# Block 1's last convolution taps beside its attentions; block 2's keys and values projected once, with the compression in the same stage

## The reference, cut to what matters

```python
def conv_branch(u_glu, u_gate, conv_w, conv_b, ln_g, ln_b, w_proj):   # block 1, beside two attentions
    a = u_glu[..., :D_CONV] * jax.nn.sigmoid(u_glu[..., D_CONV:])
    a = depthwise_conv(a, conv_w, conv_b)                             # 31 taps on 512 channels
    a = jax.nn.silu(layer_norm(a, ln_g, ln_b))
    return (a * jax.nn.silu(u_gate)) @ w_proj
...
def _compress(z, pe, w1, w2):                                         # block 2, on k_cmp and v_cmp
    zr = z.reshape(B, n_chunk, CMP_STRIDE, G, dh)
    blocks = jnp.concatenate([zr[:, j:j + nc] for j in range(r)], axis=2)
    blocks = blocks + pe[:, None, :]
    flat = blocks.transpose(0, 3, 1, 2, 4).reshape(B, G, nc, CMP_BLOCK * dh)
    return jax.nn.gelu(flat @ w1) @ w2
...
    k_cmp, v_cmp, k_slc, v_slc, k_win, v_win = [z.reshape(B, S, G, dh) for z in jnp.split(kv_a, 6, axis=-1)]
    kc = _compress(k_cmp, pe_k, ck_w1, ck_w2)
    vc = _compress(v_cmp, pe_v, cv_w1, cv_w2)
```

## Time and profile before

| | us |
|---|---|
| median of three runs | 2611.66 |
| the profiled execution | 2601.48 |
| its span | 2599.7 |
| TensorE busy | 2429.2 (93%) |
| vector engine busy | 1497.9 (58%) |
| ScalarE busy | 1252.6 (48%) |
| POOL busy | 231.9 (9%) |

### The profile page before, as it was taken

One profiled execution on the slowest core, in us unless ns is written; L12 is line 12 of the kernel. 1 busy time (PEld: TensorE's weight loads), 2 busy tenths in 40 slices (PEclk: granted clock), 3 DMA queues, 4 the chain that ended last, 5 costly groups with the idle time before them and its releaser, 6 DMA issues. The chain is left out here.

```text
span 2599.7 us, 46435 instructions
## 1 busy us (share of the span) xinstructions
PE 2429.2 (93%) x17766; PEld 2191.7 (84%) x17766; DVE 1497.9 (58%) x2660; ACT 1252.6 (48%) x1972; POOL 231.9 (9%) x228
## 2 busy tenths in 40 slices
PE   6899899999879999999989999999999989998998
PEld 5678567887767789999978789899899877898998
DVE  4489753334567755656455566554555556565554
ACT  5355654232447565433355554543543455554444
POOL 0014000000002200022000000131121000000220
PEclk8899999999989999999999999999999989999999
DMA  8221022222442035455443234455355442343553
GB/s 330 79 93 70 1 82 91 99 102 81 180 158 96 35 114 182 167 196 184 178 146 114 98 130 155 155 192 183 142 193 181 144 161 82 114 149 144 181 197 107
DMA packets 57303, 356.70 MB, mean 137 GB/s; under 512 B 5776, under 2 KB 15040, under 8 KB 15168
## 3 DMA queue, kind: packets, MB, share of 16 engines
q1 hardware_dynamic: 57008, 354.58, 38.0%
q10 hardware_dynamic: 144, 0.01, 0.0%
HBM read 353.49 MB, written 1.08 MB: 136 GB/s over the span
## 5 line engine op out<-in xcount | busy, mean ns | idle before, releaser
L259 PE MATMUL psum<-x_hi,w_hi 128*128 128x256 f32 (+1 forms) x3456 | 1061.3, 307 | 63.9 <-DVE x_lo L613 21.9
L217 DVE TENSOR_TENSOR w_lo<-ring,w_hi 128x1024 fp32r<-128x1024 f32 x652 | 824.0, 1298 | 492.3 <-ACT w_hi L205 491.9
L261 PE MATMUL psum<-x_hi,w_lo 128*128 128x256 f32 (+1 forms) x3456 | 1041.7, 301 | 0.0
L260 PE MATMUL psum<-x_lo,w_hi 128*128 128x256 f32 (+1 forms) x3456 | 1041.7, 301 | 0.0
L205 ACT ACTIVATE w_hi<-ring 128x1024 fp32r<-128x1024 f32 (+1 forms) x652 | 658.0, 1051 | 305.3 <-PE psum L1552 141.8
L259 PEld LDWEIGHTS psum<-x_hi,w_hi 128*128 128x128 f32 x3456 | 661.1, 191 | 110.9 <-issue 69.0
L260 PEld LDWEIGHTS psum<-x_lo,w_hi 128*128 128x128 f32 x3456 | 661.6, 191 | 27.7 <-issue 2.4
L261 PEld LDWEIGHTS psum<-x_hi,w_lo 128*128 128x128 f32 x3456 | 661.2, 191 | 23.8
L1552 PE MATMUL psum<-h_hi,w_lo 128*128 (+1 forms) x640 | 178.4, 279 | 0.0
L1551 PE MATMUL psum<-h_lo,w_hi 128*128 (+1 forms) x640 | 178.2, 278 | 0.0
L1549 PE MATMUL psum<-h_hi,w_hi 128*128 (+1 forms) x640 | 178.1, 278 | 0.0
(11 more groups left out here) (294 smaller groups left out, 3000.3 us busy)
## 6 DMA issues: line engine op xcount, KB each, us to landing
ring<-wstream SPq DMA_DIRECT2D x327, 1024.0 KB, 4.8
x<-xT SPq DMA_DIRECT2D x2, 1024.0 KB, 7.1
x<-ctxT SPq DMA_DIRECT2D x2, 1024.0 KB, 9.7
rel_bias<-bias_by_distance SPq DMA_DIRECT2D x2, 1024.0 KB, 7.3
cst<-consts SPq DMA_DIRECT2D x1, 1662.0 KB, 11.6
out<-x SPq DMA_DIRECT2D x8, 128.0 KB, 2.0
x<-rpb SPq DMA_DIRECT2D x2, 438.0 KB, 6.8
na_bias<-rpb SPq DMA_DIRECT2D x2, 438.0 KB, 5.4
```

What stands on the lines that cost most here:

```text
L217: dve.tensor_tensor(w_lo[:, c % 2, h], ring[:, (c + 2 * i) % RING, h], w_hi[:, c % 2, h].bitcast(F32), ALU.subtract).then_inc(split_done.s ...
L259: pe.matmul(o, w_hi[:, c, w_cols], hi, start=first, stop=False)
L260: pe.matmul(o, w_hi[:, c, w_cols], lo, start=False, stop=False)
L261: return pe.matmul(o, w_lo[:, c, w_cols], hi, start=False, stop=last)
```

## The change

Block 1. The bias is made at chunks 0 and 1 on TensorE and at j = 1 and 2 on the vector engine. The padded convolution input `cpad` stays allocated to the end of the attentions, on the other side of SBUF, and `wv` moves into the tile `rs`. A class `Conv` holds the taps. The last 32 of 124 are left for the attention, spread evenly over its steps, and `qkv_stage` now gives its last chunk a share too. (Taps behind each of the ten chunks: in layer 0 nine or ten each, before 14, 14, 13, 14, 14, 14, 13, 14, 14, 0; in layer 1 12, 11, 11, 6, 6, 6, 6, 11, 11, 12, before 18, 17, 18, 9, 9, 9, 9, 17, 18, 0.)

```diff
-                        if j % 2 == 0:
+                        if j < 2:
                             pe.wait_ge(loaded.sem, lb + 32)
-                            for h in range(2 * j, 2 * j + 4):
+                            for h in range(4 * j, 4 * j + 4):
...
-                        if j % 2:
-                            dve.wait_ge(parted.sem, f0 + j // 2 + 1)
-                            for h in range(2 * j - 2, 2 * j + 2):
+                        if j in (1, 2):
+                            dve.wait_ge(parted.sem, f0 + j)
+                            for h in range(4 * j - 4, 4 * j):
...
-            share = [0] + [t // S for _, t, _ in plan[:-1]]
-            cuts = [round(len(taps) * sum(share[:j + 1]) / sum(share)) for j in range(n)] + [len(taps)]
+            here = CONV_K * 4 - Conv.LATER
+            share = [0] + [t // S for _, t, _ in plan]
+            cuts = [round(here * sum(share[:j + 1]) / sum(share)) for j in range(n + 1)]
...
+                        cuts = [len(conv.order) - conv.LATER + round(conv.LATER * t / a.U) for t in range(a.U + 1)]
                         for t in range(a.length):
                             a.dve(dve, t)
+                            if t < a.U:
+                                conv.taps(dve, cuts[t], cuts[t + 1])
```

```diff
+            kk_sw = [sb("kk_sw", [P, 4, S], F32R, stack=st2) for _ in range(2)]
+            kks, kkw = [a[:, 0:2] for a in kk_sw], [a[:, 2:4] for a in kk_sw]
...
+                    def double(t, done):
+                        sp.dma_start(t[high, 0:4:2], t[low, 0:4:2]).then_inc(done.sem, 16)
+                        sp.dma_start(t[low, 1:4:2], t[high, 1:4:2]).then_inc(done.sem, 16)
+                    for j in range(n + m):
+                        load_one(sp, j // 2, j % 2)
+                        if j == 1:
+                            sp.wait_ge(copied.sem, c0 + 1)
+                            sp.wait_ge(acc_free.sem, g0[0] + 1)
+                            double(kv_cmp, doubled)
+                        if j == 3:
...
+                            for part in kk_sw:
+                                double(part.bitcast(F32), stored)
+                    sp.wait_ge(stored.sem, s0 + 64)
...
+                            act.activation(t[low, 0:4:2], a[low], ACT.Copy).then_inc(copied.sem, 1)
+                            act.activation(t[high, 1:4:2], a[high], ACT.Copy
+                                           ).then_inc((acc_free if kind == "kv" else upper).sem, 1)
+                        if j == 4:
+                            act.wait_ge(read.sem, rb + 16)
...
+                    for j in range(m):
+                        round_next(act, (n + j) // 2, (n + j) % 2)
+                        if j == 0:
+                            act.wait_ge(acc_free.sem, g0[0] + n)
+                            act.activation(gates[:], v_b[:, :, 128:152], ACT.Sigmoid)
...
+                    for j in range(n + m):
+                        if j:
+                            rest_next(dve, j // 2, j % 2)
+                        if j in halves:
...
+                        if j == 3:
+                            flatten()
+                        if j == 4:
+                            lower_flat()
```

More of the change, by code:

```diff
@@ L177, in build @@
         stored = count("stored")
+        copied = count("copied")
+        doubled = count("doubled")
         g0 = [0]
@@ L1216, in qkv_stage @@
             turns = (2, 5, 6)
-            taps = [(ct, k) for k in range(CONV_K) for ct in range(4)]
-            share = [0] + [t // S for _, t, _ in plan[:-1]]
-            cuts = [round(len(taps) * sum(share[:j + 1]) / sum(share)) for j in range(n)] + [len(taps)]
[L1220 to L1223, removed]
+            here = CONV_K * 4 - Conv.LATER
+            share = [0] + [t // S for _, t, _ in plan]
+            cuts = [round(here * sum(share[:j + 1]) / sum(share)) for j in range(n + 1)]
+            b, r0, w0, n0, t0, s0, f0, c0, d0 = (c.n for c in (
+                step, rooted, gpart, normed, rotated, sined, cosined, finished, read))
             def spare(e, k):
@@ L1309, in _ @@
                                               ).then_inc(sined.sem, 1)
[L1310 to L1321, removed]
+                        conv.taps(dve, cuts[j], cuts[j + 1])
                 @block.gpsimd
@@ L2077, in compress_stage, with project_and_compress @@
-        def compress_stage(layer, kv_cmp, kkc, vc, v_b, gates, st):
+        def project_and_compress(layer, plan, norm, kkc, vc, v_b, gates, st):
             flat = sb("flat", [P, 4, CMP_T // 2, NC_CMP], stack=st)
@@ L2085, in compress_stage, with result @@
             W = 2 * NC_CMP
-            n = CMP_CHUNKS
-            rb, hb, lb, b, gb = read.n, hpart.n, lpart.n, step.n, gpart.n
+            n, m = len(plan), CMP_CHUNKS
+            kv_cmp, kk_sw = plan[0][1], plan[1][1]
+            low, high = slice(0, DH), slice(DH, P)
+            u0, rb, hb, lb, b, gb = upper.n, read.n, hpart.n, lpart.n, step.n, gpart.n
+            c0, d0, s0 = copied.n, doubled.n, stored.n
+            halves = [j for j, (kind, _, _) in enumerate(plan) if kind in ("kd", "kk")]
+            def result(j):
+                wide = 2 if j == 0 else 1
+                return acc(j % 2, 512 * wide).rearrange("p (m t) -> p m t", m=2)[:, :, 0:S]
             def o_of(w):
@@ L2156, in _ @@
                 @block.tensor
                 def _(pe):
+                    for j, (kind, o, _) in enumerate(plan):
+                        if kind == "r":
+                            pe_rows(pe, j // 2, j % 2, S, o.shape[2])
+                        elif j == 0:
+                            pe_side_by_side(pe, *model_operand(S), lambda k: norm.before(pe, k))
+                        else:
+                            pe_columns(pe, j // 2, j % 2, *model_operand(S), S)
                     pe.wait_ge(lpart.sem, lb + 4)
-                    for j in range(n):
+                    for j in range(m):
@@ L2181, in compress_stage @@
+            upper.n += len(halves)
+            copied.n += 3
+            doubled.n += 32
+            stored.n += 64
             gpart.n += 1
@@ L2413, in weight_stream @@
         ffn("ffn1")
+        for pair in ((KCMP, VCMP), (KSLC, KWIN)):
+            put(_cols(w, np.concatenate([_r(c, 128) for c in pair])))
         span(w, QA, 512)
-        for c in (KCMP, VCMP, KSLC, KWIN):
-            put(_cols(w, _twice(c)))
         put(_rows(w, np.concatenate([_r(VSLC, 128), _r(VWIN, 128)])))
```

236 lines of the change are left out of this document (115 added, 121 removed).

## The result

The kernel after takes 2567.84 us (median of four, 2560.77 to 2570.54) against 2610.20 for the kernel before on the same chip (2606.48 to 2613.02): ratio 0.9839, 95% interval 0.9819 to 0.9859, 42.4 us faster. Forecast were 36.8. Its profiled execution took 2568.35 us.

What follows compares the result with a forecast made beforehand. TensorE, busy 93% of the span, was taken as the bound. Block 2 -34.0, block 1's bias and q/k/v taps -15.2 and taps beside attentions +12.4 sum to -36.8 us: median 2574.9, range 2556 to 2598.

Steps and rivals of the forecast that it cites:

- Block 2, -34.0: Block 2's projection and compression: two of eight chunks go and the 7.86 us wait is mostly hidden, 17.0 us a layer.
- The walk: Block 2's stage stepped through on the old clock: additions to 1341.6, a 2.4 us wait, end at 1359.4 instead of 1376.24.
- The cover of the transfers: Block 2: the doubling transfers are issued 16.9 us before they are needed, so they cost zero.
- Bias, -4.2: Block 1's glu stages: bias additions moved from the stage's end to j = 2 gain 2.1 us a layer.
- Taps out of q/k/v, -8.8 and -2.2: Block 1's q/k/v stages keep 92 of 124 taps: shorter TensorE waits and clock gains, 8.8 us in layer 0, 2.2 in layer 1.
- upper bound: Block 1's bias and q/k/v taps: at most 21 us, from 4.2, waits of 2.23, 6.19 and 3.77, and 4 of clock.
- Beside the attentions, +12.4: Block 1's attentions: 32 taps each fill the vector engine, costing 0.95 and 0.6 us a pair, 7.6 and 4.8 in all.
- Rival 1: Block 1's attentions swallow the taps in idle vector time: -49.2 us, 2562.5; chance 0.12.
- rival 2: Block 1's attentions: each tap costs its length on the loop of scores, shift and exponential, +34.6, total 2597.1; chance 0.11.
- Rival 3: Block 2's compression isn't hidden; additions, transfers or half clock give the 7.86 us back: 2586.3; chance 0.12.
- rival 4: Block 1's q/k/v rests blocked by POOL's seven multiplies a layer, 1.5 us each, 10.4 back: 2585.3; chance 0.04.
- Rival 5: Block 1's attentions: short idle times lower TensorE's granted clock, +132 us at worst, so the kernel is slower; chance 0.03.

Runs made afterwards that it cites:

- e3: Kernel after with the 16 additions of flat in two lots of eight, at j = 2 and j = 3: 2563.32 us, ratio 0.9813.
- e11: Kernel after with block 1's bias additions and clear of na_bias back at j = 1 and 3 and the stage's end: 2573.93 us, ratio 0.9866.
- e10: Kernel after run again, word for word: 2567.90 us, ratio 0.9841 to the kernel before.
- e4: Kernel after with the 92 q/k/v taps shared, more beside the first three chunks: 2560.18 us, ratio 0.9801.
- e2: Kernel after with all 124 taps back in q/k/v in the old shares, none beside the attentions: 2566.56 us, ratio 0.9843.
- e8: Kernel after with flat and both made at j = 5, behind the projection's last rest: 2571.60 us, ratio 0.9865.
- e7: Kernel after with 16 taps beside each attention instead of 32, shares and flat in two lots: 2552.40 us, ratio 0.9788.
- e9: e7 with the gates' sigmoid moved behind the compression's fourth rounding: 2554.12 us, ratio 0.9778.
- e5: Kernel after with all 124 taps in q/k/v, shared, none beside the attentions, flat in two lots: 2554.13 us, ratio 0.9797.

## Why the prediction was right

The forecast of 2574.9 lies 7.1 us above the median. 1.5 of these are the kernel before, 2610.20 here and 2611.66 in the forecast's sum; 3.1 are the terms below; the rest is not accounted for by stages. The terms, and what the experiments say of them:

- **Block 2, -34.0.** Right, -34.9. The walk ended the additions 31.8 us behind the stage's first matmul and had a wait of 2.4; they ended at 30.9, and the waits are 2.26 and 2.48. Its own end, 1359.4, lies 16.84 us before 1376.24, not 17.0, so that it gives 33.7. The four compression chunks were taken at 11.1 us and took 10.9 (1339.44 to 1350.37). The cover of the transfers was right: nothing waits for them (e3).
- **Bias, -4.2.** Right. Measured -4.8, and 4.5 in e11 against e10.
- **Taps out of q/k/v, -8.8 and -2.2.** Measured -4.95 (against -7.8: of the 8.8, 1.0 lies in the attention) and -1.9; in layer 0 the granted clock was 0.96 before and 0.98 after, which is part of it. The middle `sines` wait of layer 0 is gone as forecast, and that of layer 1 fell from 3.77 to 2.59. The mis-sized term is "these end some 2 us after TensorE instead of 6: gain 3.5". They end 4.5 us after TensorE, the wait is 4.78 and the gain 1.4: the nine taps started 2.6 us before TensorE's end and took 7.06 us, not 6.1, since the second of them met POOL's last sum and took 1.76 instead of 0.74. (By the prediction's own 6.19 less 2 the gain would have been 4.2, not 3.5, and its upper bound adds up to 20.4, not 21.) The share of the last chunk was the weak point of the change (e4: 3.8 us of it at no cost). The first scores behind the wait, counted at +1.0 gained, were no faster (0.52 of the clock).
- **Beside the attentions, +12.4.** Measured +6.6. The step that failed is "so the vector engine becomes the bound" with 11.2 and 6.7 as what the filled engine needs and some idle time on top. It did fill, from the third pair to the last but one with less than 0.1 us of idle time in each, but at 10.7 to 10.8 and up to 6.5: tails of instructions that stood alone before were counted in full, though work that follows at once covers them. The pairs together cost 1.6 us and the starts and ends 5.1, where the forecast had 0.95 and 0.6 for every one of the eight. Rival 1 (all swallowed, 0) and rival 2 (+34.6) both fall.
- **Taps in sum:** forecast +1.4, measured -0.2 by the two profiles, +2.5 by e2's, some -3 by all eight profiles with these shares (e2). The gain and the cost were both forecast too large, and that they cancelled is luck.
- **Rival 3** falls with e3 and e8, and **rival 4** with e4: rests beside POOL's multiply take 3.8 us in it too, and TensorE idles 0.9 us in its whole layer 0 stage. One such rest does hold TensorE, in layer 1's q/k/v stage, but in the kernel before as well: 1.72 us there, 1.53 after. **Rival 5:** the clock over layer 0's attention is 0.93 after, 0.97 in e2, but it fell only in the first pair; from the second on it is 1.00. What the Trainium skill (TensorE: Matmul & The Clock Gate, "A second HAM failure mode: psum-queue depth-cycling") tells of another kernel, frequent small idle times that keep switching the clock, isn't seen here: the waits of 0.6 to 0.7 us at every pair of layer 0, which the kernel before had too, left it there. In layer 1 the clock fell within the first two pairs in five of six profiles with 32 taps and in one of four with none, never later; whether the taps bring that about stays open. The window of layer 0 from the second pair on, in the kernel after:

```profile
271.96:352.68 80.72, 73.34 (x658) 46.61 (x657) 76.51 (x279) 60.34 (x146) 0.00 (x0) 1.00 0.00 1
```

## What to carry to other kernels

Before work goes into a later stage, look for idle time at the front of the stage where it is: here the vector engine idled 7.6 us before each of two rests at the start of q/k/v, and shares that use it took 3.8 us of waiting out of layer 0 (e4), where moving 32 taps gave nothing that the medians show. Work shared evenly over chunks should leave the last one short if a stage's end waits for it. For an engine that will be full, add distances from start to start, not busy times; up to the point where its idle time is used up such filler costs little (in layer 1 0.8 us for 16 taps in e7, 1.5 in e9), and more behind it (2.9 to 4.6 us for 32 in six profiles, the slow start included). And read the granted clock beside a stage's time before two profiles of it are compared: the same code took 106.0 and 108.9 us.

## What the runs showed of the hardware

TensorE ran at two paces at a granted clock of 1.00. The same last ffn stage, a window of 100 us in the profiles before and after:

```profile
2420.00:2520.00 100.00, 100.00 (x885) 100.00 (x884) 59.61 (x57) 43.50 (x56) 30.87 (x38) 1.00 0.55 195
2390.00:2490.00 100.00, 100.00 (x851) 100.00 (x850) 57.63 (x53) 42.03 (x54) 29.29 (x36) 1.00 0.53 187
```

885 matmuls against 851, 113 ns from one to the next against 118. In this stage the profiles of the kernel before and of e5 ran at 113, the other eleven at 118; e10 ran at 113 for some 125 us in the middle of block 2 (1633 to 1759) instead, where the first profile of the same kernel ran at 118. So it belongs to the execution, not to the kernel. From the start of this stage to the end it makes 7.05 us (198.64 before, 205.69 after), which covers the 6.8 by which the untouched stages seem longer after, and much of why the spans differ by 33.1 and the medians by 42.4. What sets it stays open.

The clock moves whole runs too. Of 23 runs of the kernel before, the thirteen at a mean granted clock of 0.970 or less have a median of 2611.0 us, the ten at 0.971 or more one of 2606.1. That difference is as large as any net effect of the tap move, in the medians as in the stages, and so its sign is not shown.
